# Moving quarters, transposes, one silu and the norm's ends in a hand-written order of work

## The reference

```python
def second_block(x, p, g_pre, w_in, ...):
    u = _rms_norm(h, g_pre[i])
    cols = u @ w_in[i]                       # q k v z of the attention, r k v z of the recurrence, gates
    y_a = _moba_attention(qa, ka, va, rel_bias) * silu(za)        # 8 heads of 64, softmax over 256 keys
    y_b, z_b = _rwkv7_time_mix(b_cols, ...)  # a recurrence over 256 positions, then a norm per head:
    #   y = (y - mean) * rsqrt(var + GN_EPS) * ln_w + ln_b + bonus
    y_b = y_b * silu(z_b)
    merged = sigmoid(gate_a) * (y_a @ p_a) + sigmoid(gate_b) * (y_b @ p_b)
    y = merged @ w_out[i]
    h = h + _rms_norm(y, g_post[i])
    h = h + sigmoid(h @ w_ple_gate[i]) * (p[i] @ w_ple_up[i])
```

## Time and profile before

| what | value |
|---|---|
| three runs | 885.73, 888.42, 888.45 us, median 888.42 |
| profiled execution | 884.25 us, of which 882.2 us is the span from first to last instruction |
| PE matmul busy | 861.0 us, 98% of the span |
| DVE busy | 669.9 us, 76% |
| ACT busy | 480.5 us, 54% |
| POOL busy | 119.8 us, 14% |
| mean granted PE clock | 0.996 |

### The profile page before, as it was taken

The page is one execution under the profiler, slowest core; times in us unless marked ns, Lnnn a source line. Parts: engine busy times, 40 slices in busy tenths (PEclk is TensorE's granted clock), DMA queues, the critical chain, the costliest instruction groups (busy, mean ns, idle before and its releaser), DMA issues. The chain is left out here.

```text
span 882.2 us, 19228 instructions
## 1 busy us (share of the span) xinstructions
PE 861.0 (98%) x7612; PEld 786.7 (89%) x7612; DVE 669.9 (76%) x996; ACT 480.5 (54%) x775; POOL 119.8 (14%) x136
## 2 busy tenths in 40 slices
PE   7999999999999999999999999999999989898998
PEld 7999888888889988888888888899999979797998
DVE  6996887777667876778877767786998676567775
ACT  5774565555445576655555554459613554373463
POOL 2003300000122000050000017630007200000110
PEclk9999999999999999999999999999999999998999
DMA  9542555554556533155555455674443543333451
GB/s 341 193 169 104 171 187 186 185 188 142 189 196 224 192 116 111 61 191 191 190 190 188 163 162 183 214 271 144 144 144 100 136 130 94 124 114 138 140 195 48
DMA packets 23410, 144.50 MB, mean 164 GB/s; under 512 B 2968, under 2 KB 3224, under 8 KB 9648
## 3 DMA queue, kind: packets, MB, share of 16 engines
q1 hardware_dynamic: 22032, 140.26, 46.2%
q0 software_dynamic: 1168, 3.23, 1.6%
q10 hardware_dynamic: 144, 0.06, 0.0%
HBM read 142.47 MB, written 1.06 MB: 163 GB/s over the span
## 5 line engine op out<-in xcount | busy, mean ns | idle before, releaser
L2150 DVE TENSOR_TENSOR lo<-raw,hi 128x1024 fp32r<-128x1024 f32 (+1 forms) x210 | 244.1, 1205 | 11.4 <-ACT hi L1540 8.3
L609 PE MATMUL ps<-X,hi 128*128 128x512 f32 x704 | 221.1, 395 | 0.0
L596 PE MATMUL ps<-X,hi 128*128 128x256 f32 x600 | 173.1, 289 | 0.2
L597 PE MATMUL ps<-X,hi 128*128 128x256 f32 x600 | 169.7, 283 | 0.0
L598 PE MATMUL ps<-X,lo 128*128 128x256 f32 x600 | 169.7, 283 | 0.0
L606 PEld LDWEIGHTS ps<-X,lo 128*128 128x128 f32 x704 | 132.0, 188 | 33.4 <-issue 1.9
L606 PE MATMUL ps<-X,lo 128*128 128x256 f32 x704 | 139.5, 279 | 1.1 <-DVE X L2165 1.0
L1540 ACT ACTIVATE hi<-raw 128x1024 fp32r<-128x1024 f32 (+1 forms) x109 | 107.7, 988 | 27.1 <-DMA raw<-in_down 13.6
L596 PEld LDWEIGHTS ps<-X,hi 128*128 128x128 f32 x600 | 114.9, 191 | 3.8 <-issue 2.7
L597 PEld LDWEIGHTS ps<-X,hi 128*128 128x128 f32 x600 | 115.0, 192 | 0.4 <-issue 0.2
L598 PEld LDWEIGHTS ps<-X,lo 128*128 128x128 f32 x600 | 115.0, 192 | 0.0
(11 more groups left out here) (443 smaller groups left out, 1442.3 us busy)
## 6 DMA issues: line engine op xcount, KB each, us to landing
raw<-in_wide SPq DMA_DIRECT2D x106, 1024.0 KB, 5.0
raw<-in_down SPq DMA_DIRECT2D x32, 704.0 KB, 4.1
BI<-bias_table POOLq DMA_DIRECT2D x16, 128.0 KB, 5.1
raw<-in_wide SPq DMA_DIRECT2D x3, 512.0 KB, 8.6
X<-in_x SPq DMA_DIRECT2D x1, 1024.0 KB, 12.7
WG<-in_group SPq DMA_DIRECT2D x1, 768.0 KB, 16.9
out<-X SPq DMA_DIRECT2D x3, 256.0 KB, 2.4
cmask<-in_masks POOLq DMA_DIRECT2D x1, 544.0 KB, 6.3
```

Of the source, the lines that this page charges most:

```text
L596: nc.tensor.matmul(dst, wh, xh, start=first, stop=False, skip_group_check=True)
L597: nc.tensor.matmul(dst, wh, xl, start=False, stop=False, skip_group_check=True)
L609: return nc.tensor.matmul(bank, wh, x, start=False, stop=last, skip_group_check=True)
L2150: nc.vector.tensor_tensor(lo[:, s, a:b], raw[:, s, a:b], hi[:, s, a:b].bitcast(F32), ALU.subtract).then_inc(lo_ready, 1)
```

## The change

Four edits, all in the order of steps:

1. In slots 11, 12, 14 and 15 two quarters are taken where three were (13 and 16 had two already). The four quarters that this leaves over are taken behind the slots.
2. Where a slot takes a third quarter, it now stands behind `mturn` (the transposes) and not ahead of it. This matters in slots 8 and 10.
3. The silu of the attention's second half of z, and `z_silu`, go from slot 8 to the end of slot 10. A silu and an exp need different tables in ACT, so this adds a table load for each direction.
4. Behind the slots, `gn3` and `gn4` go from their places between the halves of units 127 and 128 to places between the quarters that were held back. `gate_sig` is cut 4 and 4 and not 5 and 3.

```diff
-        SHARE = {0: 4, 13: 2, 16: 2}
+        SHARE = {0: 4, 11: 2, 12: 2, 13: 2, 14: 2, 15: 2, 16: 2}
...
-            second += quarters(2) + turned_in.get(n, []) + quarters(share - 2)
+            second += quarters(2) + turned_in.get(n, [])
             if n in TURNS:
                 p = TURNS.index(n)
                 second += [("mturn", 2 * p), ("mturn", 2 * p + 1)]
+            second += quarters(share - 2)
...
-            if n == 8:
+            if n == 10:
                 second += [("z_silu",)]
-        second += converted() + [("gate_sig", 0, 5)] + quarters(1)
+        second += converted() + [("gate_sig", 0, 4)] + quarters(1)
         second += both_groups("gn") + [("p_load",)] + converted() + quarters(3) + both_groups("gn2") + [("own_out",)] + converted()
-        second += quarters(len(fills_)) + converted() + [("gate_sig", 5, 8)]
-        for half in range(2):
-            second += [("fill", U_PA, half)]
-        second += [("gn3", 0), ("gn4", 0), ("fill", U_PA + 1, 0), ("gn3", 1), ("gn4", 1), ("p_in",), ("fill", U_PA + 1, 1)]
+        second += quarters(3) + [("gn3", 0)] + converted() + quarters(3) + [("gn4", 0), ("gn3", 1)] + converted()
+        second += quarters(len(fills_)) + [("gn4", 1)] + converted() + [("gate_sig", 4, 8)]
+        for u in (U_PA, U_PA + 1):
+            for half in range(2):
+                second += [("fill", u, half)] + ([("p_in",)] if (u, half) == (U_PA + 1, 0) else [])
...
-                if half and part != 0 and U_ZA <= u < U_GATE:
-                    j = u - U_ZA
-                    act.wait_ge(za_in, j + 1)
-                    z = ZA[:, 2 * j:2 * j + 2, :]
-                    nc.scalar.activation(z, z, ACT.Silu).then_inc(za_done, 1)
+                if half and part != 0 and u == U_ZA:
+                    gate_silu(0)
+
+            def gate_silu(j):
+                act.wait_ge(za_in, j + 1)
+                z = ZA[:, 2 * j:2 * j + 2, :]
+                nc.scalar.activation(z, z, ACT.Silu).then_inc(za_done, 1)
...
             def z_silu():
                 act.wait_ge(shifted, 5)
+                gate_silu(1)
                 nc.scalar.activation(C[:, 12:16, 1:], C[:, 12:16, 1:], ACT.Silu).then_inc(z_done, 1)
```

## The result

The changed kernel takes 878.9 us, the median of four runs (877.37 to 879.68); the kernel before took 887.28 beside it, the median of four (885.73 to 888.45). The ratio is 0.9906, with a 95% interval of 0.9885 to 0.9927. The profiled execution took 878.52 us.

The account below looks back on a forecast made before the run. PE was taken to bound the kernel, busy 861.0 of 882.2 us. Terms 1.5 + 0.24 + 6.0 - 0.3 - 1.1 gave 6.4 us less, so a median of 882.0 us; range 879.0 to 886.8.

Parts of the forecast that it names:

- Slots 8 and 10: Quarters behind the transposes and the later silu start the product with the values earlier: gains 1.5 and 0.24 us.
- The second silu, price 0: End of slot 10: ACT's extra table load and silu delay a copy by 0.2 us, covered by PE's quarters; cost 0.
- Two quarters for three: Slots 11, 12, 14, 15: moved work costs 0; a new wait of 0.3 us at `sa` in slot 14.
- Behind the slots, 6.0 less 1.1: After the slots: the `YBH` wait of 3.69 and its clock tail go, 6.0 us; new wait at unit 128, 1.1.
- DVE's sum: Behind the slots: DVE needs 22.5 us to its product, PE is ready at 21.4, so PE waits 1.1 at unit 128.
- the clock's 2.35: Behind the `YBH` wait: 25 matmuls take 5.47 us at half clock, 3.12 at full; the change gains this 2.35 us.
- The first rival: Behind the `YBH` wait: the 2.35 us clock gain doesn't come; gain 4.05, time 884.4 us, chance 0.16.
- a wait of 2.10 left the clock alone: Slot 9: PE's wait of 2.10 us had no half-clock tail; argued against the clock gain failing to come.
- The second rival: Unit 128: DVE's longer list makes PE wait 3.7 us, clock falls; gain 1.45, time 887.0 us, chance 0.13.
- The third: Slots 11 to 15: DVE and ACT set the pace, waits 6.7 us in all; 1.7 slower, 890.1 us, chance 0.09.

Follow-up runs that it names:

- before with the busy start: Kernel before the change, with six matmuls on constants of 128 columns added among the first unit's products: 884.02 us, ratio 0.9984.
- the last two orders: Changed kernel, second gate_sig behind unit 128's first half, six start matmuls: 875.39 us; also three quarters in slots 13 and 15, norm ends moved: 874.77 us.

## Why the prediction was right in kind and too small in size

- **Slots 8 and 10.** 1.47 and 0.17 for 1.5 and 0.24. The prices were right. What was not seen is that in slot 8 edit 2 gives nothing without edit 3: a quarter moved behind the transposes only makes PE wait later while the silu stands ahead of the copies.
- **The second silu, price 0.** Right, by the rows of slot 10.
- **Two quarters for three.** Right: a wait of 0.20 at `sa` for 0.3, none in slot 12, and the two waits of 0.84 unchanged. But "as work that is 4 x 1.50 out and 4 x 1.50 in, 0" overlooked that PE's list changes its place by 48 matmuls against the stall in `yt`. This is the first step that failed: the term was put at 0 and was worth 1.14 us. I had searched PE's waits by a named releaser, passed over the row with "issue", and never set the stretch's length against its neighbours.
- **Behind the slots, 6.0 less 1.1.** Right for this pair of traces: 4.93 in the terms of the sum. DVE's sum held part by part: counted from PE's 778.18, which answers to 784.56 before, the last gate is taken by 17.2 (17.3 forecast), its product starts 4.4 later (4.45), and PE begins to wait at 21.4 (21.4). But the clock's 2.35 is one draw and not a price. Behind the same wait the 25 matmuls lost 2.35 in before, 1.42 with edits 2 and 3 alone, and 4.39 - 3.12 = 1.27 in before with the busy start. That the term came out in full owes something to luck.
- **The first rival, "the clock's share doesn't come".** It came. But the argument against it, "a wait of 2.10 left the clock alone", failed on the chip: the same wait had a half-clock stretch behind it in the experiment with edits 1 and 4. This is the second step that failed, and it matters for the base. By the traces of before's variants such stretches stand behind the wait in slot 9, behind `YBH` and at the start, in changing number; the changed kernel's two traces have only the start's left. So I take it that the change takes away more clock, on the whole, than the one profiled execution shows.
- **The median.** The profiled pair differs by 884.25 - 878.52 = 5.73, which is the 7.59 of the stage less the 1.89 of a start at half clock. The medians differ by 8.4. Of the 882.0 - 878.9 = 3.1 that the forecast is too high, 1.1 is the base (888.42 of three runs, 887.28 of four), 1.1 is the stall, and the remaining 0.8 I put down to the half-clock stretches that before has more often. That last share is inferred from the mean clocks, not measured by itself; it is no larger than what runs of one kernel differ by at the same mean clock. Against its 23 neighbours the changed kernel's second median is 885.96 - 878.09 = 7.9 less.
- **The second rival**, a longer DVE list at unit 128: the wait is there at 1.1, all of it gone when the sigmoids are moved, and far from the 3.7 that it speaks of. **The third**, exposed slots: 0.20 and 0.84 twice, nowhere near 6.7.
- **The range.** Its low end was the full gain with no new wait, 9.45 less than the median. It had no room for a loss in before that the list of waits doesn't hold, nor for the clock behind the wait in slot 9. The stall's 1.14 alone would have moved it to 877.9.

## What to carry to other kernels

When one engine is busy 98% of the time, list everything that it does not run at full pace: waits by releaser, stalls with no releaser (compare the length of like stretches), and windows with a lower granted clock; in the stage the waits gave 1.64 - 0.20 + 3.69 - 1.11 = 4.0 us here, the stall and the clock together 1.14 + 2.35 = 3.5. When a stall has no releaser, count its place in the engine's list and look for an instruction packet just ahead of it; if both fit, any edit that moves the list can win or lose it, and the gain isn't the edit's own. Work held back as cover is only worth something where another engine's late step stands beside it, so move the two together and look at every step behind the new place, ACT's table loads included. And where one profiled execution is all there is, a stretch at full clock behind a wait is no evidence that the wait leaves the clock alone.

## What the runs showed of the hardware

- **Stalls tied to a place in PE's list.** In `yt` PE stood still for 0.84 and 1.39 us behind matmul 117 of 128 in two kernels with as many matmuls up to there, for 1.04 behind 105 with 12 more in the list, for 0.71 behind 118 in the changed kernel with 48 put in, and not at all in the kernels with 12 to 48 fewer. Another place is ahead of four small matmuls at 644.49 before and 646.38 after, 0.67 in both. There it was 1.30 and 0.33 in other kernels with the same list up to there, none with edit 3 undone, and none in the kernels with 12 or 48 more. So the place is fixed and the size is not. All lie in or beside runs of 64 x 64 matmuls, some 60 of them in a microsecond.
- **The supply of instructions is what stalls.** All 16 stalls stand 117 or 118 entries beyond a multiple of 256 in PE's list and end 2.26 to 2.56 us behind the start of a packet of 16,384 bytes on the instruction queue. At entry 9333 PE ran through in seven kernels, and there it came 3.1 us or more behind the start of the packet. What sets the size of a stall, 0.33 to 1.39 us at one place, was not found.
- **The clock behind waits.** Behind each of the five waits of 3.6 to 3.7 us for `YBH` in the traces the clock stood at 0.50, for 6.8 us in two of them and for 3.4 in three. Behind a wait of 2.4 and one of 1.97 it did so too, behind one of 1.48 (in two traces) and one of 1.39 it did not, and behind the wait of 2.0 to 2.1 in slot 9 in two traces of four. At the start it fell behind waits of 0.70 and 0.87 us in the changed kernel's trace and not behind 1.37 and 1.43 in that of before. With edit 4 undone two stretches cost 3.3 us. Filling the start with six matmuls of 128 columns kept the mean clock at 0.999 or 1.000 in six runs of six, and in all ten of the last two orders as well; 24 of one column did not.
